# Attention work gathered into one insertion before every third projection pair, with the context moved to bank 7's upper half

## What is computed

```python
x = x + FFN_HALF * swiglu(rmsnorm(x, ffn1_norm[l]), ffn1_w_gate[l], ffn1_w_up[l], ffn1_w_down[l])
h = rmsnorm(x, mix_norm[l])
proj = h @ w_in                      # (256 x 1024) @ (1024 x 5888)
qa, ka, va, qb, kb, vb, qc, kc, vc, gate_logits = jnp.split(proj, points, axis=-1)
q, k = rope(rmsnorm_per_head(q)), rope(rmsnorm_per_head(k))
ya = moba_attention(qa, ka, va) @ w_branch_a            # 4 heads of 64, causal
yb = sliding_window_sink_attention(qb, kb, vb, sinks) @ w_branch_b   # 4 query, 2 key heads
oc = differential_attention(q1, q2, k1, k2, vc, lam)    # 4 heads, values 128 wide
yc = (rmsnorm(oc, diff_subln) * (1.0 - lam_init)) @ w_branch_c
merged = gates[:, :, 0] * ya + gates[:, :, 1] * yb + gates[:, :, 2] * yc
x = x + merged @ w_out
x = x + FFN_HALF * swiglu(rmsnorm(x, ffn2_norm[l]), ffn2_w_gate[l], ffn2_w_up[l], ffn2_w_down[l])
```

## Time and profile before

| what | value |
|---|---|
| median of 3 runs | 1161.25 us (1161.24 to 1161.34) |
| profiled execution, its own time | 1161.08 us |
| span of the profiled execution | 1159.3 us |
| TensorE busy with matmuls | 1148.8 us, 99% of the span, 5963 instructions |
| VectorE busy | 779.6 us, 67% |
| ScalarE busy | 639.9 us, 55% |
| GpSimd busy | 72.1 us, 6% |
| 16 DMA engines | 207.34 MB, mean 179 GB/s |
| granted TensorE clock | 9 in all 40 slices (90% of full speed or more) |

### The profile page before, as it was taken

The page is one execution under the profiler, slowest core; times in us unless marked ns, Lnnn a source line. Parts: engine busy times, 40 slices in busy tenths (PEclk is TensorE's granted clock), DMA queues, the critical chain, the costliest instruction groups (busy, mean ns, idle before and its releaser), DMA issues.

```text
span 1159.3 us, 16118 instructions
## 1 busy us (share of the span) xinstructions
PE 1148.8 (99%) x5963; PEld 961.0 (83%) x5963; DVE 779.6 (67%) x1072; ACT 639.9 (55%) x936; POOL 72.1 (6%) x81
## 2 busy tenths in 40 slices
PE   8999999999999999999999999999999999999998
PEld 6888888888778888888888888888887888888887
DVE  4766657778857676566677656668687495766655
ACT  6545545657773565455555544556576745555542
POOL 3200000221100000000040000002110000000000
PEclk9999999999999999999999999999999999999999
DMA  9955554454534665556567555536445545656520
GB/s 312 287 192 197 188 185 146 161 167 146 171 136 166 218 218 182 183 184 193 175 156 240 188 182 184 188 103 216 146 153 174 180 142 188 218 186 194 190 84 37
DMA packets 138364, 207.34 MB, mean 179 GB/s; under 512 B 6818, under 2 KB 99028, under 8 KB 138292
## 3 DMA queue, kind: packets, MB, share of 16 engines
q1 hardware_dynamic: 137444, 205.55, 53.8%
q0 software_dynamic: 752, 0.79, 0.8%
q10 hardware_dynamic: 96, 0.02, 0.0%
HBM read 205.29 MB, written 1.05 MB: 178 GB/s over the span
## 4 chain that ended last, share of the span: by engine, by line
PE 96%; ACT 1%; DVE 1%; DMA 1%; issue 0%; SPq 0%; ACTq 0%; DVEq 0%
PE bank L521 27%; PE bank L489 17%; PE bank L493 16%; PE bank L492 16%; PE bank L525 14%; PE bank L503 1%; DMA raw<-in_ffn_w_up 1%; PE bank L705 1%; PE bank L675 1%; PE bank L691 1%; PE bank L690 1%; PE bank L722 1%; DVE probs L1258 0%; DVE oT_low L1097 0%; ACT w_high L843 0%
## 5 line engine op out<-in xcount | busy, mean ns | idle before, releaser
L1086 DVE TENSOR_TENSOR w_low<-raw,w_high 128x1024 fp32r<-128x1024 f32 x388 | 470.7, 1231 | 299.8 <-ACT w_high L843 299.2
L843 ACT ACTIVATE w_high<-raw 128x1024 fp32r<-128x1024 f32 x388 | 403.9, 1056 | 334.1 <-PE bank L525 172.4
L521 PE MATMUL bank<-xT,w_high 128*128 128x512 f32 x1392 | 492.2, 398 | 2.5 <-DVE work L1120 2.0
L525 PE MATMUL bank<-xT,w_low 128*128 128x256 f32 x1408 | 390.3, 280 | 0.0
L521 PEld LDWEIGHTS bank<-xT,w_high 128*128 128x128 f32 x1392 | 261.2, 188 | 67.5 <-issue 2.1
L525 PEld LDWEIGHTS bank<-xT,w_low 128*128 128x128 f32 x1408 | 263.8, 189 | 1.4
L489 PE MATMUL bank<-w_high,xT 128*128 128x512 f32 (+1 forms) x448 | 177.1, 395 | 0.1
L493 PE MATMUL bank<-w_low,xT 128*128 128x512 f32 (+1 forms) x448 | 171.6, 383 | 0.0
L492 PE MATMUL bank<-w_high,xT 128*128 128x512 f32 (+1 forms) x448 | 171.4, 383 | 0.0
L489 PE MATMUL bank<-w_high,oT_high 128*128 128x512 f32 x416 | 163.6, 393 | 0.0
L493 PE MATMUL bank<-w_low,oT_high 128*128 128x512 f32 x416 | 162.6, 391 | 0.0
(11 more groups left out here) (129 smaller groups left out, 748.1 us busy)
## 6 DMA issues: line engine op xcount, KB each, us to landing
raw<-in_w_in SPq DMA_DIRECT2D x92, 512.0 KB, 4.5
raw<-in_ffn_w_down SPq DMA_DIRECT2D x88, 512.0 KB, 4.2
raw<-in_ffn_w_gate SPq DMA_DIRECT2D x87, 512.0 KB, 4.0
raw<-in_ffn_w_up SPq DMA_DIRECT2D x87, 512.0 KB, 5.0
raw<-in_w_out SPq DMA_DIRECT2D x16, 512.0 KB, 4.4
raw<-in_w_branch_c SPq DMA_DIRECT2D x8, 512.0 KB, 4.3
raw<-in_w_branch_b SPq DMA_DIRECT2D x4, 512.0 KB, 6.3
raw<-in_w_branch_a SPq DMA_DIRECT2D x4, 512.0 KB, 4.7
```

The lines of the kernel that those rows point to most:

```text
L521: return nc.tensor.matmul(bank[n][:, :], w_high[:, slot, column(k, n)], xT[:, k], start=k == 0, stop=False)
L525: return nc.tensor.matmul(bank[n][:, 0:S], weights[:, slot, column(k, n)], xT_high[:, k], start=start, stop=k == KB - 1)
L843: act.activation(w_high[:, slot], raw[:, in_slot, (p % 2) * 1024:(p % 2) * 1024 + 1024], ACT.Copy).then_inc(sem["high_ready"], 1)
L1086: dve.tensor_tensor(w_low[:, slot], raw[:, FILL_SLOT[p // 2], (p % 2) * 1024:(p % 2) * 1024 + 1024], w_high[:, slot].bitcast(F32), ALU.sub ...
```

## The change

The three pieces of attention work that lay before three different pairs now lie before one. At m = 16, 19, 22, ... TensorE does the scores of the unit whose position it is, then the context of the unit two before, then the turn of the unit one before. TURN_AFTER is 3 instead of 4 and CONTEXT_AFTER is 6 instead of 5. The turned rotations of chunks 3 and up move from m = 25 and 31, where they stood with scores, to 26 and 32, where they stand alone; VectorE's rotations move from 22, 29 and 33 to 25, 32 and 35, and their squares from 21, 28 and 32 to 23, 31 and 34. The turn of the outputs of C moves from 37 to 40 and from banks 6 and 7 to banks 4 and 5. The context now goes to the upper half of bank 7. Of a unit of A or B, the six turned blocks lie in bank 6 (four) and in the lower half of bank 7 (two). The context and some of the turned blocks then share bank 7, and `read_context` and `context_low` get waits that keep their reads of it out of the time in which TensorE turns into that bank. The instructions are the same in number and size, except for the split of the turned blocks (256 and 512 columns instead of twice 384).

```diff
-ROPE_TURNS = [(0, 4, 10), (4, 4, 15), (8, 4, 25), (12, 3, 31)]
-O_TURN = 37
+ROPE_TURNS = [(0, 4, 10), (4, 4, 15), (8, 4, 26), (12, 3, 32)]
+O_TURN = 40
-TURN_AFTER, CONTEXT_AFTER = 4, 5
+TURN_AFTER, CONTEXT_AFTER = 3, 6
-        GROUP_BANKS = {ST_FFN1: (4, 5, 6, 7), ST_MIX: (2, 3, 2, 3), ST_O: (6, 7, 6, 7), ST_MERGED: (2, 3, 2, 3), ST_FFN2: (4, 5, 6, 7)}
+        GROUP_BANKS = {ST_FFN1: (4, 5, 6, 7), ST_MIX: (2, 3, 2, 3), ST_O: (4, 5, 4, 5), ST_MERGED: (2, 3, 2, 3), ST_FFN2: (4, 5, 6, 7)}
-        SQUARES_AT = {0: 9, 1: 13, 3: 21, 4: 28, 5: 32}
-        ROPE_AT = {0: 10, 1: 14, 3: 22, 4: 29, 5: 33}
+        SQUARES_AT = {0: 9, 1: 13, 3: 23, 4: 31, 5: 34}
+        ROPE_AT = {0: 10, 1: 14, 3: 25, 4: 32, 5: 35}
-        SUBLN_AT = 35
+        SUBLN_AT = 37
...
                     pe.wait_ge(sem["context_read"], value("context_read", layer, {2: 2, 3: 4}[n]))
+                    pe.wait_ge(sem["probs_copied"], value("probs_copied", layer, {2: 3, 3: 5}[n]))
...
                 pe.wait_ge(sem["probs_ready"], value("probs_ready", layer, u + 1))
-                if u > 0:
-                    pe.wait_ge(sem["context_read"], value("context_read", layer, u))
-                if u == 6:
-                    pe.wait_ge(sem["blocks_low"], value("blocks_low", layer, banks_split(ST_O, 0, 1)))
...
-                        last = nc.tensor.transpose(bank[6 + t][:, b * P:(b + 1) * P], probs_of[u % 2][:, t, b * P:(b + 1) * P], ident[:, :])
+                        n = 3 * t + b
+                        last = nc.tensor.transpose(bank[6 + n // 4][:, n % 4 * P:n % 4 * P + P], probs_of[u % 2][:, t, b * P:(b + 1) * P], ident[:, :])
...
                 pe.wait_ge(sem["probs_copied"], value("probs_copied", layer, u + 1))
+                if u > 0:
+                    pe.wait_ge(sem["context_read"], value("context_read", layer, u))
+                pe.wait_ge(sem["rope_copied"], value("rope_copied", layer, sum(pos < UNITS[u][3] + CONTEXT_AFTER for _, _, pos in ROPE_TURNS)))
+                out = bank[7][:, S:2 * S]
...
+                        if m == pos + CONTEXT_AFTER:
+                            context(layer, u)
                         if m == pos + TURN_AFTER:
                             turn_probs(layer, u)
-                        if m == pos + CONTEXT_AFTER:
-                            context(layer, u)
...
                         pe.wait_ge(sem["subln_ready"], value("subln_ready", layer, 1))
-                        pe.wait_ge(sem["context_read"], value("context_read", layer, 6))
+                        pe.wait_ge(sem["scores_masked"], value("scores_masked", layer, 8))
                         turn_group(layer, ST_O, 0, o_nat)
...
             def read_context(layer, u):
                 act.wait_ge(sem["context_done"], value("context_done", layer, u + 1))
+                if u + 1 < 8 and UNITS[u + 1][0] != "C":
+                    act.wait_ge(sem["probs_turned"], value("probs_turned", layer, u + 2))
...
+                        if m == pos + CONTEXT_AFTER + RING - 1:
+                            read_context(layer, u)
                         if m == pos + TURN_AFTER + RING - 1:
                             copy_probs(layer, u)
-                        if m == pos + CONTEXT_AFTER + RING - 1:
-                            read_context(layer, u)
...
                 dve.wait_ge(sem["context_high"], value("context_high", layer, u - 3))
+                if u + 1 < 8:
+                    dve.wait_ge(sem["probs_copied"], value("probs_copied", layer, u + 2))
```

More of the change, by code:

```diff
@@ L711, in context @@
                 pe.wait_ge(sem["probs_copied"], value("probs_copied", layer, u + 1))
+                if u > 0:
+                    pe.wait_ge(sem["context_read"], value("context_read", layer, u))
+                pe.wait_ge(sem["rope_copied"], value("rope_copied", layer, sum(pos < UNITS[u][3] + CONTEXT_AFTER for _, _, pos in ROPE_TURNS)))
+                out = bank[7][:, S:2 * S]
                 if kind == "C":
-                    out, c0 = bank[7], 384 + u * P
+                    c0 = 384 + u * P
                     pT, v = probsT[:, 0], values[:, :, c0:c0 + P]
@@ L721, in context @@
                             c0 = (2 * (u - 4) + t) * DH if kind == "A" else 256 + t * DH
-                            last = nc.tensor.matmul(bank[6][t * DH:t * DH + DH, queries], values[:, half, c0:c0 + DH], probsT[:, t, keys],
+                            last = nc.tensor.matmul(out[t * DH:t * DH + DH, queries], values[:, half, c0:c0 + DH], probsT[:, t, keys],
                                                     start=half == 0, stop=half == 1)
@@ L764, in branches @@
                 p = BRANCH0
-                pe.wait_ge(sem["scores_masked"], value("scores_masked", layer, 8))
+                pe.wait_ge(sem["blocks_low"], value("blocks_low", layer, banks_split(ST_O, 0, 1)))
                 pe.wait_ge(sem["context_read"], value("context_read", layer, 8))
@@ L998, in copy_probs @@
                 act.wait_ge(sem["probs_turned"], value("probs_turned", layer, u + 1))
-                for t in range(1 if UNITS[u][0] == "C" else 2):
-                    last = act.activation(probsT[:, t], bank[6 + t][:, 0:3 * P], ACT.Copy)
+                flat = probsT[:, :, :].rearrange("p t k -> p (t k)")
+                for first, b, width in ((0, 6, 3 * P),) if UNITS[u][0] == "C" else ((2 * S, 7, S), (0, 6, 2 * S)):
+                    last = act.activation(flat[:, first:first + width], bank[b][:, 0:width], ACT.Copy)
                 last.then_inc(sem["probs_copied"], 1)
@@ L1005, in read_context @@
                 act.wait_ge(sem["context_done"], value("context_done", layer, u + 1))
+                if u + 1 < 8 and UNITS[u + 1][0] != "C":
+                    act.wait_ge(sem["probs_turned"], value("probs_turned", layer, u + 2))
                 if UNITS[u][0] == "C":
                     c0 = context_column(u)
-                    act.activation(o_nat[:, :, c0:c0 + P], bank[7][:, 0:S].rearrange("p (t c) -> p t c", t=2), ACT.Copy
+                    act.activation(o_nat[:, :, c0:c0 + P], bank[7][:, S:2 * S].rearrange("p (t c) -> p t c", t=2), ACT.Copy
                                    ).then_inc(sem["context_read"], 1)
                 else:
-                    act.activation(oT_high[:, context_block(u), :], bank[6][:, 0:S], ACT.Copy).then_inc(sem["context_high"], 1)
+                    act.activation(oT_high[:, context_block(u), :], bank[7][:, S:2 * S], ACT.Copy).then_inc(sem["context_high"], 1)
             def mixing(layer):
@@ L1308, in context_low @@
                 dve.wait_ge(sem["context_high"], value("context_high", layer, u - 3))
-                dve.tensor_tensor(oT_low[:, block, :], bank[6][:, 0:S], oT_high[:, block, :].bitcast(F32), ALU.subtract
+                if u + 1 < 8:
+                    dve.wait_ge(sem["probs_copied"], value("probs_copied", layer, u + 2))
+                dve.tensor_tensor(oT_low[:, block, :], bank[7][:, S:2 * S], oT_high[:, block, :].bitcast(F32), ALU.subtract
                                   ).then_inc(sem["context_read"], 1)
```

## The result

The changed kernel takes **1175.45 us** (median of 4 runs, 1174.68 to 1176.6), the kernel before beside it 1161.24 (1161.12 to 1161.34). The ratio is 1.0123, with a 95% interval of 1.011 to 1.0136: slower by 14.2 us. The forecast was 1170.3 us with a range up to 1174.5. The sign and the places were right, the size was 5 us too small, and the result lies 0.95 us above the range.

What follows compares the result with a forecast made beforehand. TensorE's standing still was taken as the bound. Each layer: + 0.7 + 3.35 + 2.4 - 1.1 - 0.85 = 4.5 us; both layers' 9.0 us on the 1161.25 us median gave 1170.3 us, range 1165.2 to 1174.5.

Steps and rivals of the forecast that it cites:

- scores of unit 3 wait for the mask of unit 2: TensorE, three pairs after pair 22: scores due at 275.8 wait for VectorE's mask to 276.5, 0.7 us a layer.
- turn of unit 2 waits for its probabilities: TensorE before pair 25: turn due at 278.05 waits for VectorE's normalised probabilities to 281.4, 3.35 us a layer.
- old waits gone: TensorE's waits before the turn of unit 6 and the context of unit 0 vanish, saving 1.1 us a layer.
- gathering: TensorE's insertions from pair 16 on: twelve boundaries fewer at 0.07 save 0.85 us a layer, bounds 0 and 1.2.
- The bound: TensorE carries 96% of the last-ending chain and hardly waits in mixing, so each microsecond it stands still longer lengthens the kernel.
- second stall: TensorE before pair 32 waits for VectorE's last rotation, via pair 36's high or via first stall's lag: 2.4 us a layer.
- first stall: TensorE's waits on unit 2 before pair 25, for its mask 0.7 us and its probabilities 3.35 us, in each layer.
- The clock falls in the stall: Rival: TensorE drops to half clock for one to three pairs a layer, 1175.7 to 1186.5 us; chance 0.08.
- the prediction's own sign of being wrong: A granted clock below 1.00, or a first insertion before pair 25 starting by 278 and ending by 279.
- one stall alone: Rival: only the wait before pair 25 comes, 1165.4 us, or only that before pair 32, 1162.2 us; chance 0.10.
- Faster: Rival: engines reach the third rotation early enough that no turn waits, winning 3.9 us, 1157.4 us; chance 0.06.
- The change does not do what it says: Rival: the gaps in TensorE's work are only moved and the waits cancel, 1161 us; chance 0.03.

Runs made afterwards that it cites:

- e1_fill: The changed kernel with matmuls of zeros in both stalls, 12 before the turn of unit 2 and 8 before the last rotation's turn: 1170.85 us.
- e4_turn1: The changed kernel with VectorE's rotations at 22, 31, 34 (squares 21, 30, 33) and the turn of unit 1 alone one pair later: 1158.87 us.
- e5_mask: e4_turn1 with VectorE's mask of unit 1 ahead of the third rotation instead of behind it: 1158.03 us.
- e3_last: The changed kernel with VectorE's last two rotations and their squares one number earlier, the third rotation staying at 25: 1168.87 us.
- e2_rot: The changed kernel with VectorE's rotations and their squares back at the places of the kernel before: 1164.17 us.
- e6_read5: The changed kernel with ScalarE's reads of projection 5 behind the exponentials of unit 2 instead of ahead of them: 1169.89 us.
- e8_fillA: e1_fill with only the 12 fillers before the turn of unit 2, the 8 before the last rotation's turn left out: 1172.33 us.

## Why the prediction was wrong by its size

By its own steps, with the changed kernel and e1_fill as measure:

| Term, one layer | Predicted | Measured |
| --- | --- | --- |
| scores of unit 3 wait for the mask of unit 2 | +0.7 | +0.8 |
| turn of unit 2 waits for its probabilities | +3.35 | +3.5, +3.2 (3.3 and 3.0 idle) |
| last rotation before pair 32 | +2.4 (1.8 to 3.0) | +2.8, +2.5 |
| old waits gone | -1.1 | -1.1 (both are gone; their price is that of the kernel before) |
| gathering | -0.85 | about -0.9 |
| mixing, both layers, full clock | +9.0 | +9.5 (e1_fill: 5.04 and 4.50) |
| clock, both layers | 0 | **+4.6** |

- **The bound** was read rightly: each microsecond of TensorE's standing still came through. The chain carried forward by hand met the trace closely: mask of unit 2 done at 276.45, measured 276.84; turn due at 278.05 and freed at 281.4, measured about 278.6 and 282.1. Of these shifts 0.4 us lies at the start of the program, ahead of mixing. The other 0.3 us before the release is a handover that the prediction left out: VectorE ends the rotation at 275.24 and ScalarE starts its reads at 275.62. A small slip, mask to exponentials as 1.65 where 264.35 to 266.06 is 1.71, moves nothing.
- **The second stall** was taken at 2.4 and measured 2.5 to 2.8. Of its two paths the second, over the first stall, came last. ScalarE of the changed kernel has no gap from the exponentials of unit 4 to the high of pair 35, and for that high VectorE's low waits:

```profile
302.28 0.40 ACT L993 ACTIVATE probs<-probs,stats 128x128 f32<-128x128 f32 x1 [4.55 <-DVE stats L1277]
...
306.64 1.05 ACT L845 ACTIVATE w_high<-raw 128x1024 fp32r<-128x1024 f32 x1
...
307.73 1.22 DVE L1092 TENSOR_TENSOR w_low<-raw,w_high 128x1024 fp32r<-128x1024 f32 x1 [0.54 <-ACT w_high L845]
```

The high of pair 36, at which the first path was to end, is done at 309.67, before VectorE comes to it at 309.95; the low in the middle of the rotation does not wait for it.

- **Gathering** was right in size, by a part that the prediction undersized. It took 0.06 from the insertions themselves and 0.01 for the slower steps behind them. Between pairs 12 and 46 of the kernel before, 126 steps last over 0.2295 us instead of 0.227, and in e4_turn1 62 to 65. That is 0.82 us of excess against 0.40, so 0.04 us for each boundary lies in these steps. By the rule that the prediction worked out from the Trainium skill (page "TensorE: Matmul & The Clock Gate", section "LDWEIGHTS (loading the stationary operand)") the gathering would be worth nothing; e4_turn1 measures 0.9 us a layer, and the measurement decides.
- **The failed step is the price of the clock, which the sum put at nothing.** The prediction wrote "The clock falls in the stall" as a rival with a chance of 0.08, although its condition, a stall of over 3 us on TensorE where none in the attention part had been over 0.4, was the forecast itself. A consequence of the likeliest case is a term of its sum, not another case. It came true beside both stalls, as the prediction's own sign of being wrong, a clock below 1.00, shows (0.994 to 0.997 in the four runs). It cost 4.6 us by e1_fill, somewhat less than the 5.4 to 16.2 at which the rival had it. In the profiled execution pair 25 with the turned rotation behind it took 2.2 and 1.0 us more than in e1_fill in the two layers, the transposes before it 0.25 more in each, and pair 32 of layer 1 took 1.6 more: 5.3 in all, about the rival's lower end. This execution was the slowest of the four, and the median has less of it. With the 4.6 us the sum gives 1174.9. The Trainium skill (the same page, section "HAM oscillation — how this bites in real kernels") had said that the clock falls back in idle gaps before a matmul burst, and the trace of the changed kernel agrees (0.55 from 280 to 285 us); the trace of before could show no such gap in mixing, and the silence of a trace about what it never met was taken as evidence against.
- **Other rivals**: "one stall alone" fell: both waits are in the changed kernel's list. "Faster" fell as the changed kernel stands, though its idea holds once the rotation is placed rightly: e4_turn1 and e5_mask win 2.2 and 2.9 us by the medians. "The change does not do what it says" fell by the waits.

The 0.4 us a layer that e5_mask gave back was not pursued further.

## What to carry to other kernels

When a change makes TensorE stand still in a place where it was dense, add what the clock takes behind the stall to the forecast, and let the range reach over it. When several pieces of work are gathered into one place, carry each engine's chain forward with its own order: what moved the time here was not the insertions but the rotations of VectorE, put between mask and normalisation of the next unit. Where a stall must stay, a few matmuls of zeros in it kept the clock and gave back a third of the loss.

## What the runs showed of the hardware

- **The clock falls behind short stalls, and not always.** Counting the profiled executions layer by layer: behind waits of 3.0 and 3.3 us TensorE ran part of the next pairs at 1.2 GHz 4 times of 4 (the changed kernel and e3_last). Behind waits of 2.0 to 2.8 us it did so 4 times of 10 (the changed kernel's last rotation 1 of 2, e2_rot 1 of 2, e6_read5 1 of 4, e8_fillA 1 of 2). Behind the waits of up to 0.9 us in mixing of e1_fill and e4_turn1 it never did, nor behind the wait of 1.4 us at about 25 us that every run has. What decides at 2 to 2.8 us stays open.
- **The clock splits the runs.** e2_rot ran at 1162.5 to 1163.1 us with a full clock and at 1163.9 to 1165.2 without. Its ten runs spread over 2.7 us, the 21 of the kernel before beside them over 1.2.
- **Steps behind an insertion are slow for a while.** Several matmuls of the stream behind each one last 0.231 to 0.236 us instead of 0.227. What causes it was not tried.
